# Moving one of four key products per sequence from DVE to GpSimd in a paged-cache attention

## What is computed

```
def diff_attn_sample(q, k_new, v_new, k_past, v_past, lam):
    s_past = jnp.einsum('bqhcd,bshcd->bhcqs', q, k_past) * HEAD_DIM ** -0.5
    s_new = jnp.einsum('bqhcd,bshcd->bhcqs', q, k_new) * HEAD_DIM ** -0.5
    p = jax.nn.softmax(jnp.concatenate([s_past, s_new], axis=-1), axis=-1)
    w = p[:, :, 0] - lam * p[:, :, 1]
    return (jnp.einsum('bhqs,bshe->bqhe', w[..., :P], v_past)
            + jnp.einsum('bhqs,bshe->bqhe', w[..., P:], v_new))
```

## Time and profile before

| | |
|---|---|
| median of 3 runs | 1468.37 us (1468.09 to 1469.5) |
| the profiled execution | 1468.32 us |
| its span | 1466.5 us |
| PE busy in the span | 1273.1 us (87%) |
| DVE busy | 815.9 us (56%) |
| ACT busy | 549.8 us (37%) |
| POOL busy | 21.2 us (1%) |
| DMA | 355.40 MB, mean 242 GB/s |

### The profile page before, as it was taken

How to read it: one execution, slowest core, us unless ns; L and a number is a source line. 1 busy time by engine, 2 the same in 40 slices (tenths; PEclk the granted TensorE clock), 3 DMA queues, 4 the chain that set the end, 5 groups by cost and what they waited for, 6 DMA issues and landing times.

```text
span 1466.5 us, 19316 instructions
## 1 busy us (share of the span) xinstructions
PE 1273.1 (87%) x7246; PEld 997.5 (68%) x7246; DVE 815.9 (56%) x970; ACT 549.8 (37%) x663; POOL 21.2 (1%) x26
## 2 busy tenths in 40 slices
PE   4797879899999997899877886676998999999985
PEld 1695745788888885599543443264657888888864
DVE  1436472666666632645599989366316666666334
ACT  1333224555555522353322221133125555555321
POOL 2000010000000000000000000001000000000000
PEclk9899979999999998999856556678559999999988
DMA  9939530999999966534469999853009999999200
GB/s 332 387 114 337 177 111 19 347 336 338 340 338 338 339 235 235 180 125 158 179 222 341 353 342 346 301 214 116 1 0 342 336 337 335 334 335 335 108 2 30
DMA packets 143713, 355.40 MB, mean 242 GB/s; under 512 B 4706, under 2 KB 4899, under 8 KB 143652
## 3 DMA queue, kind: packets, MB, share of 16 engines
q1 hardware_dynamic: 142388, 350.98, 67.4%
q0 software_dynamic: 1264, 3.59, 0.8%
HBM read 351.28 MB, written 3.28 MB: 242 GB/s over the span
## 4 chain that ended last, share of the span: by engine, by line
PE 74%; DVE 16%; ACT 3%; issue 2%; DMA 2%; SPq 2%; ACTq 0%; DVEq 0%
PE gu L620 24%; PE pj L391 20%; PE pj L639 16%; DVE reg L1843 3%; PE tb L425 3%; DVE wring L1840 3%; PE gu L457 2%; PE gu L807 2%; PE tb L422 2%; PE gu L809 1%; DMA wring<-in_a_w_in 1%; SPq L912 1%; PE pj L490 1%; DVE yT L1851 1%; PE pj L402 1%
## 5 line engine op out<-in xcount | busy, mean ns | idle before, releaser
L1702 DVE TENSOR_TENSOR wlo<-wring,whi 128x2048 fp32r<-128x2048 f32 x128 | 290.2, 2289 | 103.7 <-ACT whi L1233 103.6
L1233 ACT ACTIVATE whi<-wring 128x2048 fp32r<-128x2048 f32 x128 | 244.7, 1916 | 144.5 <-PE gu L620 144.5
L639 PEld LDWEIGHTS pj<-tokB,wring 128*128 128x128 f32 x2048 | 233.4, 192 | 4.7 <-issue 2.1
L639 PE MATMUL pj<-tokB,wring 128*128 128x128 f32 x2048 | 233.9, 275 | 1.7 <-issue 1.7
L1129 ACT ACTIVATE reg<-pj 128x264 f32<-128x264 f32 (+2 forms) x168 | 83.9, 510 | 365.2 <-PE pj L391 147.6
L620 PE MATMUL gu<-whi,xhi 128*128 128x512 f32 x512 | 207.7, 406 | 12.9 <-DVE xlo L1728 12.9
L620 PE MATMUL gu<-wlo,xhi 128*128 128x512 f32 x512 | 204.6, 400 | 0.0
L620 PE MATMUL gu<-whi,xlo 128*128 128x512 f32 x512 | 204.4, 399 | 0.0
L620 PEld LDWEIGHTS gu<-whi,xhi 128*128 128x128 f32 x512 | 98.2, 192 | 35.7 <-DVE xlo L1728 7.9
L620 PEld LDWEIGHTS gu<-whi,xlo 128*128 128x128 f32 x512 | 98.1, 192 | 23.2
L620 PEld LDWEIGHTS gu<-wlo,xhi 128*128 128x128 f32 x512 | 98.1, 192 | 21.6
(11 more groups left out here) (295 smaller groups left out, 1732.1 us busy)
## 6 DMA issues: line engine op xcount, KB each, us to landing
wring<-in_moe_w_gate SPq DMA_DIRECT2D x32, 2048.0 KB, 9.4
wring<-in_moe_w_up SPq DMA_DIRECT2D x32, 2048.0 KB, 10.0
wring<-in_moe_w_down SPq DMA_DIRECT2D x32, 2048.0 KB, 9.0
wring<-in_ada_w SPq DMA_DIRECT2D x24, 2048.0 KB, 13.8
wring<-in_cache_k SPq DMA_DIRECT2D x64, 512.0 KB, 5.0
wring<-in_cache_v SPq DMA_DIRECT2D x64, 512.0 KB, 5.0
wring<-in_a_w_in SPq DMA_DIRECT2D x4, 2048.0 KB, 19.9
wring<-in_a_w_out SPq DMA_DIRECT2D x2, 2048.0 KB, 16.4
```

Of the source, the lines that this page charges most:

```text
L639: m = pe.matmul(bank[:, i * P:(i + 1) * P], w[:, k, f * P:(f + 1) * P], aT[:, k, :], start=(k == 0), stop=(k == FB - 1))
L1233: act.activation(whi[q], quarter(wring, q, s), ACT.Copy).then_inc(hi_ready, 1)
L1702: dve.tensor_tensor(quarter(wlo, q, s), quarter(wring, q, s), whi[q].bitcast(F32), ALU.subtract).then_inc(lo_ready, 1)
```

## The change

DVE's fourth product of each sequence, `scores(s, 1, 1)`, loses its multiply; POOL does the same multiply in place, on the same half slot with the same broadcast query, and counts up a new semaphore `keys_times`. DVE waits for it and sums. POOL's eight products stand in its stream behind its four output stores and ahead of `clear(1)`; each waits for the spread query and for all pages of the slot.

```diff
         keys_used = sem("keys_used")
+        keys_times = sem("keys_times")
...
             pool.dma_start(o["v_sample"].rearrange("b t h e -> (b t) (h e)"), tokA[0:NB, 2, :]).then_inc(stored["vs"], 16)
+            for s in range(NB):
+                slot, count = cache_slot("k", s, 1)
+
+                pool.wait_ge(pj_evac, at[f"spread{s}"])
+                pool.wait_ge(slot_in[slot], at["cache_loads"][slot] + 16 * count)
+                keys = wring[:, slot, 2 * D:4 * D].rearrange("p (g n) -> p g n", g=2)
+                pool.tensor_tensor(keys, keys, qbc[:, s % 2:s % 2 + 1, :].to_broadcast([P, 2, D]), ALU.mult).then_inc(keys_times, 1)
             clear(1)
...
                 keys = wring[:, slot, q * 2 * D:(q + 1) * 2 * D]
-                link(dve.tensor_tensor(keys.rearrange("p (g n) -> p g n", g=2), keys.rearrange("p (g n) -> p g n", g=2),
-                                       qbc[:, s % 2:s % 2 + 1, :].to_broadcast([P, 2, D]), ALU.mult))
+                if (k, q) == (1, 1):
+
+                    dve.wait_ge(keys_times, s + 1)
+                else:
+                    link(dve.tensor_tensor(keys.rearrange("p (g n) -> p g n", g=2), keys.rearrange("p (g n) -> p g n", g=2),
+                                           qbc[:, s % 2:s % 2 + 1, :].to_broadcast([P, 2, D]), ALU.mult))
```

## The result

| | before | after |
|---|---|---|
| median | 1468.09 us (7 runs, 1465.59 to 1470.79) | 1475.79 us (7 runs, 1472.43 to 1480.83) |
| profiled execution | 1468.32 us, span 1466.5 | 1475.79 us, span 1473.9 |

The ratio is 1.0058, 95% interval 1.0036 to 1.008: slower, and above the range that was given. In the new kernel the product is line 1852, the sum 1855, POOL's product 1122, the softmax's `tensor_scalar` 1909 (1897 before), SP's pages 1042 and the ada_w tile 491.

A forecast was written before the change was run, and what follows sets the result against it. The prediction took SP's page issue as the stage's bound, DVE just behind. Its terms, -1.5 us for SP's waits and 0 for engine disturbance and run start, gave 1466.9 us; range 1464.5 to 1471.5 us.

The forecast's parts named there:

- Do the two engines disturb each other?: First sequence, POOL's product beside DVE's second: effect on the start of SP's run between -0.9 and +1.6 us, taken as 0.
- The likeliest case: The forecast itself, 1466.9 us, with no net cost from POOL and DVE overlapping; chance 0.48.
- The price of the hold: Rival: a POOL product holds DVE's next two-operand instruction until it ends; +0.1 us at a 4.4 us product, 1468.5 us; chance 0.27.
- price - 4.26: The hold rival's total change in us, where price is the POOL product's length; +0.1 at 4.4 us.
- long product: Slower rival: the same hold in the first sequence with an 8.8 us POOL product, +4.5 us, 1472.9 us; chance 0.12.
- I take -1.5: SP's unbroken page run: of 18.3 us removed from DVE, only SP's two waits for DVE's sums, 1.5 us, can go.
- PE's slack of 0.9 us: First sequence: PE is busy until 743.81, its next transpose came at 744.72, so only 0.9 of DVE's 2.29 us passes.
- The stage is bound by SP's page issue: Cache attention: SP issues a page every 1.49 us without a break at DMA share 0.98, DVE only just behind.
- the faster rival: PE's tail in the first sequence does not hold, so the start gains the whole 2.29 us: -3.8, 1464.5 us; chance 0.13.
- The wait for POOL's product: DVE's new wait before its fourth sum: POOL's product is done with 7 us and more to spare, so no cost.

The follow-up runs named there:

- e3: Kernel before with the fourth product of each sequence left out altogether, nothing on POOL: 1466.65 us, ratio 0.9986 to before.
- e4: The change, but each POOL product starts by semaphore after DVE's first product of the same sequence, sequence 0's ahead of the output stores: 1465.2 us, 0.9981 to before.
- e9: The change as it was, with SP's loop over four pages written out: 1461.51 us, ratio 0.9952 to before.
- e6: Kernel before with SP's loop over four pages written out, nothing else changed: 1464.19 us, ratio 0.9978 to before.
- e7: The gated products of e4 together with SP's page loop written out: 1450.85 us, ratio 0.9867 to the kernel before.
- e8: The change, but DVE does all four products and POOL only copies the keys onto themselves at the same place: 1471.62 us, ratio 1.0024 to before.
- e1: The change for sequences 0 and 1 alone, DVE doing all products of the other six: 1474.25 us, ratio 1.0033 to before.
- e5: The change, but sequence 1's product stays on DVE: 1469.3 us, ratio 1.0006 to the kernel before.

## Why the prediction was wrong

- *The step that failed* is "Do the two engines disturb each other?", a term that stands in the sum with 0. It measured +6.05 us (6.04 from DVE's second product on): POOL's work held DVE, and with it PE's ada_w tile and the start of SP's run. The likeliest case was that the engines don't disturb each other. I took 0 as the middle of -0.9 and +1.6 (their middle is +0.4); the row that would have settled it was not in the trace of before, and a middle between two different mechanisms is a value that neither of them gives.
- *The price of the hold*, which stood among the rivals at 0.27, was too low as well. "POOL's last issue before it ends at 728.4, so the first one is done by 732.8" counts one product. Sequence 1's keys and query were there as well, nothing else stood in POOL's queue, and the second product followed at once: 9.0 us, not 4.4. The formula of that rival, price - 4.26, gives +4.7 for 9.0; its "long product" case at 8.8 us came near by the wrong cause. Each product took 4.50 us, as sized.
- *"I take -1.5"* did not come: SP's waits for DVE went from 1.5 to 2.4 us, since DVE's later steps were held and then waited for PE. That the term was right for a DVE that really has less to do is shown by e3 and e4: run 1.5 us shorter, no wait left. From +4.7 the missing 1.5, the 0.8 by which the run grew, and 0.4 ahead of the stage lead to the 7.4 measured.
- *PE's slack of 0.9 us* held: DVE lost 9.30 - 2.28 = 7.02 us, less 0.91 is 6.11, and the stretch to the run grew by 6.05. That the two agree so closely is luck: PE's 12 matmuls behind the wait took 2.93 us at a granted clock of 0.50 instead of 2.36 at 0.64, and ada_w tile 8 took 3.06 us at 0.62 instead of 3.64 at 0.50, which cancels. In e9, with the same hold, that tile took 3.64 us, and the stretch from DVE's second product on grew by 6.57.
- *"The stage is bound by SP's page issue"* held for both kernels (1.49 us a page, (10.80 - 0.35) / 7 after the change too), and e3 showed it. Its reason, that pages can't come faster at a DMA share of 0.98, fell in e6 and e7; with it falls one of the two grounds on which the faster rival was put aside.
- *The wait for POOL's product*, the queue behind it and the stores ahead of it cost nothing, as said.

What stays open: by what rule the engine that goes first is chosen when both start within 0.2 us (POOL stood in e4's last sequence, DVE in e9 at 769.45), and whether a POOL instruction that only reads or only writes would hold DVE too. Neither was tried. The 3.6 us ahead of the stage in e8 stay unexplained.

## What to carry to other kernels

Before work is moved from DVE to GpSimd, lay the two timelines side by side: a GpSimd product or copy in SBUF stopped DVE's two-operand instructions and its `tensor_scalar` until it ended, so start it by a semaphore from DVE where DVE sums, reduces or waits. Count how many such instructions can run in a row, not what one costs. And ask of the queue that feeds the stage whether its transfers or its own instructions set the pace; only after that was changed was DVE's time worth more than some 2 us here.

## What the runs showed of the hardware that I had not expected

- The hold is a full stop and not a slowdown. In the change, e1, e5 and e8 DVE's product of 2.29 us ends 2.15 to 2.17 us after POOL's last instruction, though it began 1.9 to 2.7 us after POOL's first.
- DVE was not let in between two POOL instructions in a row (9.30 us in the change, 8.48 in e1).
- A `tensor_scalar` of 128x8 was held as well (up to 4.55 us), while sums and reciprocals never were here. And POOL can be the one that waits: 6.78 us in e4.
- A loop over registers on SP cost 0.40 us per page, 1.49 against 1.09 us written out, although the DMA share of 0.98 looked full; 411 GB/s came from the same engines.
